# Two attentions of a transformer block run inside the weight products of other branches instead of after them

## The reference, cut to what matters

```python
h = rms_norm(x, norm_mix_pre[i]);  z = h @ w_in[i]
c_q, c_kv, k_rope, q_c, k_c, v_c, g_a, g_b, g_c = jnp.split(z, split_points, axis=-1)
o_a = mla_attention(c_q, c_kv, k_rope, positions, mla_q_norm[i], w_uq[i], mla_kv_norm[i], w_ukv[i])
o_b = fourier_mix(h)
o_c = windowed_gqa(q_c, k_c, v_c, positions, gqa_sink[i])
merged = (jax.nn.sigmoid(g_a) * (o_a @ w_branch_a[i])
          + jax.nn.sigmoid(g_b) * (o_b @ w_branch_b[i])
          + jax.nn.sigmoid(g_c) * (o_c @ w_branch_c[i]))
# mla_attention: q = rms_norm(c_q) @ w_uq, 8 heads of 64 plain + 32 rotary channels;
#   kv = rms_norm(c_kv) @ w_ukv; one rotary key k_rope for all heads; softmax over all 512 keys
# windowed_gqa: 8 query heads, 2 key heads of 64 channels, a band of 128 tokens to each side, a sink
# apply_rope: (t1*cos - t2*sin, t1*sin + t2*cos) over the two halves of the rotary channels
```

## Time and profile before

| | before |
|---|---|
| runs | 3261.25, 3264.87, 3265.0 us |
| median | 3264.87 us |
| the profiled execution | 3264.1 us, of which the span is 3262.3 us |
| PE busy | 3083.3 us (95%) |
| granted TensorE clock, mean | 0.973 |

### The profile page before, as it was taken

The page is one execution under the profiler, slowest core; times in us unless marked ns, Lnnn a source line. Parts: engine busy times, 40 slices in busy tenths (PEclk is TensorE's granted clock), DMA queues, the critical chain, the costliest instruction groups (busy, mean ns, idle before and its releaser), DMA issues.

```text
span 3262.3 us, 42020 instructions
## 1 busy us (share of the span) xinstructions
PE 3083.3 (95%) x15048; PEld 2478.3 (76%) x15048; DVE 1220.6 (37%) x2009; ACT 1294.8 (40%) x2023; POOL 1493.3 (46%) x879
## 2 busy tenths in 40 slices
PE   8989998999989989998999979889999998899999
PEld 6866686888867856686888869858788876688887
DVE  5344433222053445434221070453555115645510
ACT  3353543222243353543222243464555326344421
POOL 3366454444444456355444453353444433344442
PEclk9999999999999989999999999999999998899999
DMA  3212132333322213032333322201333332233322
GB/s 124 91 46 91 39 110 79 95 96 97 103 84 84 91 33 103 23 120 78 96 96 98 102 65 92 75 1 59 96 96 96 94 93 72 74 94 96 96 92 89
DMA packets 78522, 274.37 MB, mean 84 GB/s; under 512 B 8504, under 2 KB 12216, under 8 KB 78400
## 3 DMA queue, kind: packets, MB, share of 16 engines
q1 hardware_dynamic: 74064, 266.05, 26.2%
q10 hardware_dynamic: 4336, 6.63, 0.6%
HBM read 270.54 MB, written 2.10 MB: 84 GB/s over the span
## 4 chain that ended last, share of the span: by engine, by line
PE 84%; DVE 7%; ACT 4%; issue 2%; POOL 2%; DMA 1%; DVEq 0%; ACTq 0%; SPq 0%; POOLq 0%
PE ps L583 24%; PE ps L585 24%; PE ps L584 24%; PE ps L809 3%; PE ps L822 2%; DVE HL L1587 1%; PE ps L845 1%; PE ps L948 1%; PE ps L949 1%; PE ps L950 1%; PE ps L659 1%; DVE ps L1576 1%; DVE X L1579 1%; POOL WLO L2030 1%; DMA WRAW<-wall 1%
## 5 line engine op out<-in xcount | busy, mean ns | idle before, releaser
L2030 POOL TENSOR_TENSOR WLO<-WRAW,WHI 128x1024 fp32r<-128x1024 f32 x471 | 1137.5, 2419 | 1341.0 <-ACT WHI L1114 1340.3
L583 PE MATMUL ps<-HH,WHI 128*128 128x512 f32 x2288 | 904.7, 395 | 50.9 <-DVE HL L1587 23.9
L584 PE MATMUL ps<-HL,WHI 128*128 128x512 f32 x2288 | 897.2, 392 | 0.0
L585 PE MATMUL ps<-HH,WLO 128*128 128x512 f32 x2288 | 896.9, 392 | 0.0
L1114 ACT ACTIVATE WHI<-WRAW 128x1024 fp32r<-128x1024 f32 x471 | 494.8, 1052 | 401.5 <-DMA WRAW<-wall 401.5
L583 PEld LDWEIGHTS ps<-HH,WHI 128*128 128x128 f32 x2288 | 432.9, 189 | 159.7 <-issue 23.1
L585 PEld LDWEIGHTS ps<-HH,WLO 128*128 128x128 f32 x2288 | 433.5, 189 | 92.4
L584 PEld LDWEIGHTS ps<-HL,WHI 128*128 128x128 f32 x2288 | 433.8, 190 | 87.9
L1924 DVE SCALAR_TENSOR_TENSOR ps<-U,COLS,ps 128x512 f32<-128x512 f32 x208 | 157.0, 755 | 153.9 <-ACT ps L1430 138.7
L1610 DVE TENSOR_TENSOR ACC<-ACC,SQ 128x512 f32<-128x512 f32 x80 | 73.8, 922 | 317.8 <-ACT SQ L1299 303.2
L585 PE MATMUL ps<-F2H,WLO 128*128 128x512 f32 x384 | 151.7, 395 | 0.0
(11 more groups left out here) (353 smaller groups left out, 4769.9 us busy)
## 6 DMA issues: line engine op xcount, KB each, us to landing
WRAW<-wall SPq DMA_DIRECT2D x502, 512.0 KB, 3.6
DFT<-dft ACTq DMA_DIRECT2D x4, 516.0 KB, 5.4
XROWS<-xin SPq DMA_DIRECT2D x2, 1024.0 KB, 7.2
y<-YROWS ACTq DMA_DIRECT2D x4, 512.0 KB, 2.6
PROWS<-pin ACTq DMA_DIRECT2D x2, 512.0 KB, 3.8
DIL<-dil ACTq DMA_DIRECT2D x1, 768.0 KB, 5.3
COLS<-cols ACTq DMA_DIRECT2D x1, 294.5 KB, 6.7
POSI<-posi SPq DMA_DIRECT2D x1, 256.0 KB, 11.5
```

The lines of the kernel that those rows point to most:

```text
L583: pe.matmul(out_, WHI[w_at], x_hi, start=first, stop=False)
L584: pe.matmul(out_, WHI[w_at], x_lo, start=False, stop=False)
L585: return pe.matmul(out_, WLO[w_at], x_hi, start=False, stop=last)
L2030: pool.tensor_tensor(WLO[:, s, :], whole, WHI[:, s, :].bitcast(F32), ALU.subtract).then_inc(wt_lo, 1)
```

## The change

`attention` gets a second form, `carried`, in which its pairs are woven into a host stage.

- The gqa attention is carried by `fourier_branch`. The stage has 19 steps. Step q makes the scores of pair q, the value products of pair q - 3, and turns pair q - 2. In even steps up to 14 a gate tile is made (two of its 8 parts before the turning, six after it), in odd ones the mirrored tile. Steps 16 and 17 hold the first gate tile of the `branch` stage that comes next (`begun`).
- The mla attention is carried by a new stage `branch_mla` of 19 steps, which holds the six other tiles of o_c: half a gate tile, half a gate tile, and a tile over the four tiles of OC, in turns.
- The scores have one pair of PSUM banks (4 and 5) instead of two, the value products one bank, and the tiles rotate over three banks instead of four. The turned probabilities have 4 slots instead of 8. Results of the groups wait in `OCR`, `OCR2`, `OAR` (copied by DVE, `heads_out`) and are split at the stage's end (`heads_hi`, `heads_lo`), since the operand's place is still in use by the host.
- The gates in the host stages are made with Tanh (x 0.5, then (1 + t) x 0.5) instead of Sigmoid.
- The squares of CQ, their sum, factors and rows (`cq_square`, `cq_sums`, `cq_spread`) are made inside `fourier_branch`. The operand stages of CQ keep the rounding and the remainder.
- `w_uq` is packed with the rotary columns of each head twice, the second time with the halves exchanged, so each head's product has 128 rows; the rows 64 to 127 of RBQ are multiplied once with a table that holds the cosine and the signed sine. The keys hold the rotated `k_rope` twice. The scores contract over 128 rows. What is left of `rope` is the key's part, and it stands ahead of `mla_heads`.

```diff
-            u.append(("w_uq", l, 0, Q_LORA, n * 2 * MLA_QK, 2 * MLA_QK))
+            u.append(("w_uq doubled", l, 0, Q_LORA, n * 2 * MLA_QK, 2 * P))
...
         f = add("fourier", tiles=2 * ST + 2 * FGROUPS + 1, per={"channels_transformed": 8, "tokens_transformed": 9, "operand_hi_ready": 8, "dft_loaded": 32, "nyquist_cleared": 2, "nyquist_loaded": 16}, op=op, made=start, l=l)
-        fb = add("fourier_branch", units=2 * DT, tiles=3 * DT, per={"weights_folded": 2 * DT, "gate_ready": DT, "unfolded": DT, "product_ready": DT}, made=f)
-        fb.att = attention("gqa", GQA_H // 2, "OC", l=l, proj=pr)
+        cq = add("cq_norms", per={"cq_square_ready": QT + 1, "cq_square_added": QT - 1, "cq_summed": 1, "cq_mean_ready": 2, "cq_factors_ready": 1, "cq_spread": 2, "cq_rows_ready": 2}, proj=pr)
+        fb = add("fourier_branch", units=2 * DT, tiles=4 * DT, per={"weights_folded": 2 * DT, "gate_ready": DT, "unfolded": DT, "product_ready": DT}, made=f)
+        attention("gqa", GQA_H // 2, "OC", l=l, proj=pr, made=fb)
         fb.tables = tables
         need_oc = need(GQA_H // 2)
-        operand("CQ", "CQ", f"mla_q_norm{l}", QT, True, made=pr)
-        nq = norm("Q", Q_LORA, "inner")
-        operand("CQ", "CQ", f"mla_kv_norm{l}", 1, True, t=QT, made=pr)
-        nk = norm("K", KV_LORA, "inner")
+        fb.cq = cq
+        operand("CQ", "CQ", f"mla_q_norm{l}", QT, False, made=pr)
+        operand("CQ", "CQ", f"mla_kv_norm{l}", 1, False, t=QT, made=pr)
         need_cq = need(QT + 1)
-        branch(GQA_H // 2, "OC", False, False, need_oc, (nq, nk), reps=1)
-        heads = add("mla_heads", units=5, tiles=20, per={"part_multiplied": 4 + 11}, op=need_cq)
-        rp = add("rope", tiles=MLA_H + 1, per={"rope_rotated": 9, "cos_applied": 9, "rope_added": 9, "rope_keys_spread": 1}, proj=pr, heads=heads)
-        branch(GQA_H // 2, "OC", False, False, need_oc, reps=3, t=2)
-        attention("mla", MLA_H // 2, "OA", l=l, rope=rp)
+        fb.proj = branch(GQA_H // 2, "OC", False, False, need_oc, reps=1)
+        fb.proj.begun = True
+        rp = add("rope", tiles=1, per={"rope_rotated": 1, "cos_applied": 1, "rope_added": 1, "rope_keys_doubled": 1, "rope_keys_spread": 1}, proj=pr)
+        heads = add("mla_heads", units=5, tiles=20, per={"part_multiplied": 4 + 11, "rope_scaled": 1}, op=need_cq, made=cq)
+        bm = add("branch_mla", units=2 * (DT - 2), tiles=16, per={"gate_ready": DT - 2, "product_ready": DT - 2}, kt=GQA_H // 2, src="OC", op=need_oc, t=2)
+        attention("mla", MLA_H // 2, "OA", l=l, rope=rp, made=bm)
+        bm.att.qk = heads
         branch(MLA_H // 2, "OA", False, True)
...
+            def fourier_branch(st):
+                att, after = st.att, st.proj
+                attention_ready(att)
+                for q in range(att.heads * ST + DEPTH + 1):
+                    n, odd = divmod(q, 2)
+                    if q < att.heads * ST:
+                        scores(att, q)
+                    if q > DEPTH:
+                        value_products(att, q - DEPTH - 1)
+                    if n < DT and not odd:
+                        tile_part(st, 2 * n, 3 * n, pair["H"], DT, 0, 2)
+                    if DEPTH <= q < att.heads * ST + DEPTH:
+                        turn(att, q - DEPTH)
+                    if n < DT and not odd:
+                        tile_part(st, 2 * n, 3 * n, pair["H"], DT, 2, DT)
+                    elif n < DT:
+                        mirrored(st, n)
+                    elif q == 2 * DT:
+                        tile_part(after, 0, 0, pair["H"], DT, 0, 3)
+                        cq_sums(st.cq, att)
+                    elif q == 2 * DT + 1:
+                        tile_part(after, 0, 0, pair["H"], DT, 3, DT)
+                cq_spread(st.cq)
+
+            def cq_sums(st, att):
+
+                pe.wait_ge(*scores_free(att, att.heads * ST))
+                pe.wait_ge(S["cq_square_added"], st.at("cq_square_added", QT - 1))
+                pe.wait_ge(S["cq_square_ready"], st.at("cq_square_ready", QT + 1))
+                for x, at in ((ACC[:, :], 0), (SQ[:, 0, :], ST)):
+                    for s in range(ST):
+                        mm = pe.matmul(ps[4][:, at + s:at + s + 1], x[:, s * P:(s + 1) * P], ONES[:, 0:1], start=True, stop=True)
+                mm.then_inc(S["cq_summed"], 1)
+
+            def cq_spread(st):
+
+                pe.wait_ge(S["cq_factors_ready"], st.at("cq_factors_ready", 1))
+                for bank, at in ((5, 0), (4, ST)):
+                    for s in range(ST):
+                        mm = pe.transpose(ps[bank][:, s * P:(s + 1) * P], RC["Q"][:, at + s:at + s + 1].to_broadcast([P, P]), IDENT[:, :])
+                    mm.then_inc(S["cq_spread"], 1)
 
...
+                pr = st.proj
+                pe.wait_ge(bank_free[st.bank(0)], st.use(0))
+                pe.wait_ge(bank_free[pr.bank(10)], pr.use(10) + 1)
+                pe.matmul(ps[st.bank(0)][0:MLA_QK, :], ROT[MLA_NOPE:MLA_QK, :], KRAW[MLA_NOPE:MLA_QK, :],
+                          start=True, stop=True).then_inc(S["rope_rotated"], 1)
...
+            def branch_mla(st):
+                att = st.att
+                attention_ready(att)
+                pe.wait_ge(S["operand_ready"], st.op + st.kt)
+                for q in range(att.heads * ST + DEPTH + 1):
+                    r, part_ = divmod(q, 3)
+                    if q < att.heads * ST:
+                        scores(att, q)
+                    if q > DEPTH:
+                        value_products(att, q - DEPTH - 1)
+                    if DEPTH <= q < att.heads * ST + DEPTH:
+                        turn(att, q - DEPTH)
+                    if r < DT - 2 and part_ < 2:
+                        tile_part(st, 2 * r, 2 * r, pair["H"], DT, 4 * part_, 4 * part_ + 4)
+                    elif r < DT - 2:
+                        tile_part(st, 2 * r + 1, 2 * r + 1, pair[st.src], st.kt, 0, st.kt)
 
...
+            def fourier_branch(st):
+                att = st.att
+                for q in range(att.heads * ST + DEPTH + 1):
+                    n, odd = divmod(q, 2)
+                    if q < att.heads * ST:
+                        exponentials(att, q)
+                    if DEPTH <= q < att.heads * ST + DEPTH:
+                        turned_copies(att, q - DEPTH)
+                    if q < 2 * DT:
+                        split_of(st, q)
+                    if q <= QT:
+                        cq_square(st.cq, q)
+                    if n < DT and not odd:
+                        act.wait_ge(bank_free[st.bank(3 * n)], st.use(3 * n) + 1)
+                        act.activation(GT[:, :], GT[:, :], ACT.Tanh, scale=0.5).then_inc(S["gate_ready"], 1)
+                    elif n < DT:
+                        k = 3 * n + 2
+                        act.wait_ge(unit_used, st.unit(2 * n + 1) + 1)
+                        if n >= 2:
+                            act.wait_ge(bank_free[st.bank(k - 7)], st.use(k - 7) + 1)
+                        act.activation(TM[:, n % 2, 0:UH], ps[st.bank(k)][:, 0:UH], ACT.Copy, scale=0.5).then_inc(bank_free[st.bank(k)], 1)
+                heads_hi(att, unit_used, st.unit(2 * DT - 1) + 1)
...
+            def heads_hi(att, done, at):
+
+                act.wait_ge(done, at)
+                for g in range(att.heads):
+                    if g < att.heads - 1:
+                        act.wait_ge(bank_free[att.made.heads_bank()], att.made.heads_use(g) + 1)
+                    else:
+                        act.wait_ge(S["pair_multiplied"], att.at("pair_multiplied", 4 * g + 4))
+                    x = raw_heads(att, g) if g < att.heads - 1 else out_bank(att, g)[:, :]
+                    act.activation(pair[att.out][0][:, g, :], x, ACT.Copy).then_inc(S["operand_hi_ready"], 1)
...
+                dve.wait_ge(S["cq_rows_ready"], st.made.at("cq_rows_ready", 2))
+                at = slice(MLA_NOPE, P)
+                dve.tensor_tensor(RBQ[at, :], RBQ[at, :], COS[at, :], ALU.mult).then_inc(S["rope_scaled"], 1)
+                dve.wait_ge(S["rope_scaled"], st.at("rope_scaled", 1))
...
+                dve.wait_ge(S["rope_rotated"], st.at("rope_rotated", 1))
+                dve.tensor_tensor(TM[at, 0, :], ps[st.bank(0)][at, :], SIN[at, :], ALU.mult).then_inc(bank_free[st.bank(0)], 1)
+                dve.tensor_tensor(KRAW[at, :], KRAW[at, :], COS[at, :], ALU.mult).then_inc(S["cos_applied"], 1)
+                dve.wait_ge(bank_free[st.bank(0)], st.use(0) + 1)
+                dve.wait_ge(S["cos_applied"], st.at("cos_applied", 1))
+                dve.tensor_tensor(KRAW[at, :], KRAW[at, :], TM[at, 0, :], ALU.add).then_inc(S["rope_added"], 1)
+                dve.wait_ge(S["rope_added"], st.at("rope_added", 1))
+                dve.tensor_copy(KRAW[MLA_QK:P, :], KRAW[at, :]).then_inc(S["rope_keys_doubled"], 1)
...
+            def fourier_branch(st):
+                att = st.att
+                pool.wait_ge(S["table_stepped"], st.tables.at("table_stepped", 16))
```

(64 more changed lines are left out.)

559 lines of the change are left out of this document (307 added, 252 removed).

## The result

| | before | after |
|---|---|---|
| median | 3263.06 us (4 runs, 3260.64 to 3265.0) | 3189.86 us (4 runs, 3188.47 to 3190.48) |
| ratio | | 0.9774, 95% interval 0.9762 to 0.9787 |
| the profiled execution | 3264.1 us, span 3262.3 | 3190.5 us, span 3188.6 |
| mean granted clock | 0.973 | 0.977 |

The change makes the kernel 73.2 us faster. Some of the 13 is the starting point, as the median of before is now 3263.06 and was 3264.87 when the forecast was made; the gain itself is 12 us larger than forecast. The 0.14 us alone would mean nothing (the four runs of after spread over 2 us), the 12 do.

A forecast was written before the change was run, and what follows sets the result against it. PE was taken as the bound (84% of the chain), losing time to idling and a halved clock; 3264.1 - 71.9 removed + 10.4 at joints = 3202.6, forecast 3203 us, range 3190 to 3236.

The forecast's parts named there:

- Rival 3: Its own statement is missing from the text; forecast together with rival 1 at 3212 to 3258 us, chance 0.25.
- Rivals 1 and 2: Queues late in every host step, 3222 or 3241 us, 0.25 with rival 3; VectorE and GpSimd contention, 3278 us, 0.09.
- the floor: From Fourier branch through mla attention, PE never waiting at full clock: 263.6 us a layer, 71.9 us saved in all.
- rival 5: Better than forecast: no waiting at the joints and none of the half clock, 3193 us or less; chance 0.05.
- joints at nothing, and 2 us of scaling error in the floor: Basis of the range's lower end, 3190 us: no new PE waits between stages, and a floor off by 2 us.
- the joints: Places between and at starts of stages where PE waits anew: 5.2 us a layer, 10.4 in all, between 0 and 25.
- The floor's gqa pair: Gqa in the Fourier host: 0.625 of an mla pair's 3.77 us by keys, so 2.35 us, 37.6 for 16.
- The fourth unit of the short stage: Short o_c stage: unit ready after 10.2 us, PE there after 8.3, so 1.9 us of waiting, between 0 and 3.
- The clock after it: Half clock behind the short o_c stage's wait: 1.7 us a layer, between 0 and 3.4.
- The fourth unit of the heads: Heads stage: unit ready after 14.6 us, PE there after 13.4, so 1.2 us of waiting, between 0 and 4.4.
- The rest: Starts, with a table load ahead of mla's first exponentials: 0.4 us a layer, between 0 and 1.5.
- The mla term: Mla attention stage: 67.1 us less 60.3 of PE work, so 6.8 us a layer lost and to be regained.

The follow-up runs named there:

- bias run: Each gqa bias tile made twice on POOL, against the kernel after: 3189.53 us, ratio 0.9776.
- same-half run: Both heads of a gqa pair read query and key rows from the same partition half, against the kernel after: 3205.81 us, ratio 0.9828.
- the run made for it: Three more ACT copies of 512 columns ahead of the rounding of the short o_c stage's fourth unit, against the kernel after: 3191.67 us, ratio 0.9784.
- mla apart: Mla attention in a stage of its own behind six uncarried o_c tiles, against the kernel after: 3196.13 us, ratio 0.9801.
- 96-row run: Scores over the first 96 of 128 rows, against the kernel with mla apart: 3199.75 us, ratio 0.9806.

## Why the prediction was right in kind and off in size

**The mechanism** held: both attentions, the norms and rope left the path, PE never starved in the hosts, and the clock stayed at 1.00. The mla host took 110.5 us against 110. Rival 3 fell with the rows: one table load of 1.28 us in each host. Rivals 1 and 2 have nothing in the waits, and the bias run shows that there was slack left. The weaving paid what the floor said, and more; the case that came true is rival 5, which had a chance of 0.05.

**The failed step is the one that set the range's lower end: "joints at nothing, and 2 us of scaling error in the floor".** The stretch was to last 263.6 + 5.2 = 268.8 us a layer and lasted 262.6, below the floor itself. Of these 6.2 us, 4.1 lie in the joints (1.07 us a layer for 5.2) and 2.1 in a floor that was too high:

- *The floor's gqa pair, "0.625 of that: 2.35 us".* The Fourier host took 113.3 us for 116.5. Less the Fourier branch (70.4), a gate tile (5.5) and the sums and spread (2.5, for my 3.0), 34.9 are left, 2.18 a pair. I scaled a pair of mla by its keys, and so missed that gqa's heads lie in different row halves and their scores overlap. The value matmuls that I compared work with all 128 rows in both attentions and couldn't show it; the scores in the same chain of before, 0.85 us, could. The same-half run shows the overlap, 16 to 17 us over both layers, and also that scaling by columns is itself too cheap: without overlap a score group takes 1.06 and 1.49 us, where it gave 0.86 and 1.29. That a pair came out no further off is luck: its scores take 0.74 us on average for my 1.08, but the pair 2.18 for 2.35, so its other pieces cost more than scaled and took back half. That is 2.7 us a layer, with 0.5 more from the sums; the short stage, the heads and the mla host took 1.1 more than the floor gave them. The pair alone, 5.4 us in both layers, is over the 2 us that I allowed.
- *The fourth unit of the short stage, 1.9.* It waited 0.93. The four roundings and two rows on ACT took 3.5 us for 4.2, and the last remainder on DVE some 0.8 for 1.2; a table load of 1.28 us on ACT, which I hadn't seen coming, fell into the wait for DVE.
- *"The clock after it", 1.7.* It never fell, not behind 0.93 us nor behind 2.12 in the run made for it. In the kernel before the norms lost their clock over three waits (1.27, 1.36 and 1.35 us, of which I counted two) and 16 records of one-column sums in 24.1 us; I carried half of that loss to one wait.
- *The fourth unit of the heads, 1.2.* No wait. POOL had its three remainders done in 7.1 us from 251.65 on, ahead of PE. The bound of nothing was the right one.
- *The rest*, 0.4 for mla's start, came to 0.14.

Over both layers that is 8.3 us in the joints and 4.2 in the floor, 12.5 together, for the 12 us by which the gain was larger than forecast.

**Contention of DVE and POOL** came out other than weighed, and the trace says why. Groups by form of the Fourier host after, for DVE's fold, POOL's probabilities, and DVE's product:

```profile
L1794 DVE TENSOR_TENSOR WF<-WRAW 128x512 f32<-128x512 f32 x14 | 11.5, 858 | 2.6 <-DMA WRAW<-wall 2.6
...
L2344 POOL TENSOR_SCALAR SG<-SG,RS 128x384 f32<-128x384 f32 x10 | 7.9, 801 | 2.5 <-DVE RS L2008 2.5
...
L1819 DVE SCALAR_TENSOR_TENSOR MG<-GT,MG 128x512 f32<-128x512 f32 x8 | 5.8, 730 | 0.1
```

The fold rose from 679 ns to 858, far from the 1992 that I gave it as a worst case, and POOL's scaling from 584 to 801. The product fell from 1992 to 730. Which POOL instruction runs beside it decides. A product before, with POOL; a product after, with POOL; and, also after, the cosine product of the key and the sum behind it, with POOL:

```profile
143.79 1.84 DVE L1659 TENSOR_TENSOR MG<-MG,SG 128x512 f32<-128x512 f32 x1
142.67 2.41 POOL L2030 TENSOR_TENSOR WLO<-WRAW,WHI 128x1024 fp32r<-128x1024 f32 x1 [1.01 <-ACT WHI L1114]
...
154.43 0.72 DVE L1819 SCALAR_TENSOR_TENSOR MG<-GT,MG 128x512 f32<-128x512 f32 x1
154.03 2.10 POOL L2344 TENSOR_SCALAR SGX<-SGX,RS 128x384 f32<-128x384 f32 x2 [0.27 <-DVE RS L2008]
...
243.42 2.17 DVE L1958 TENSOR_TENSOR KRAW<-KRAW,COS 32x512 f32<-32x512 f32 x1
245.69 0.68 DVE L1961 TENSOR_TENSOR KRAW<-KRAW,TM 32x512 f32<-32x512 f32 x1
234.81 10.23 POOL L2262 TENSOR_TENSOR WLO<-WRAW,WHI 128x1024 fp32r<-128x1024 f32 x4 [10.86 <-ACT WHI L1216]
```

Before, all seven products of the earlier trace rows began while a remainder of POOL ran, which reads two tensors, and took 1.82 to 2.40 us. After, seven of the eight met only POOL's scaling, which reads one, and took 0.67 to 0.72; the eighth shared its first 0.44 us with a remainder and took 0.99. The new form of the product (one scalar and two tensors) isn't needed to explain it: after, too, a product of two tensors took 2.17 us beside a remainder, and the sum of the same shape 0.68 once POOL had stopped at 245.04. So what I wrote down as the price of POOL's work is that of its remainders, the folds beside its scaling and bias tiles rose by a quarter only, and by luck the weaving parted the products from the remainders. POOL was busy for 80.9 us where the sums of before gave 69.4, still 71% of the stage.

**Credits, part by part** (us over both layers, forecast and run): gqa 21.0 and 23.7; norms 14.6 and 16.7; rope 21.6 and 22.7; mla 13.6 and 6.3. The joints, forecast at 10.4 and found at 2.1, are no item beside these: each run already has the joints that its order leaves. The mla term was right as the loss of the old stage and wrong as a gain of *carrying*. From before to after, the six o_c tiles and mla together went from 49.77 + 67.09 us to 110.52, 6.3 a layer for my 6.8 less 0.4 at the start. But the separate stage with the wider tiles lasts 64.4 us and not 67.1, as the halved clock is gone there too. So of 12.7 us in both layers 7.1 come with the carrying (the stretches with mla apart), 3.6 with the step from 96 to 128 rows, and some 2 are in neither: the stages of before, 67.1 us in both layers, are that much longer than the 66.9 and 65.4 of the 96-row run, almost all in layer 1, where the clock stayed low for longer.

## What to carry to other kernels

Weaving a latency-bound attention into a stage of plain products gives back idle time and clock together; the floor (the stage's own work on PE, at full clock) is then a good forecast, if the slack of the other queues is counted per step. Take such a floor from rows of the very matmuls, which the trace of before often has, and scale only between matmuls of the same geometry: a pair of operands in different row halves is cheaper than its columns say. Price a joint at the wait that the queues give, and add the clock only where the rows show it behind a single wait of that kind, with the same shapes ahead of it. Price the meeting of two engines by the pair of instructions that will meet, not by how busy the other engine is.

## What the runs showed of the hardware

- Two float32 score matmuls over 64 rows, one in each half of the rows: 0.84 us with 384 columns each, against 1.49 in the same half; 0.63 with 256 columns, against 1.06.
- A VectorE product of two float32 tensors in SBUF, 512 columns: 1.82 to 2.40 us when begun beside GpSimd's subtraction of two tensors, 0.67 to 0.72 (in the form with a scalar) beside its scaling of one tensor. On 32 partitions 2.17 us beside the subtraction, where a sum of the same shape took 0.68 with GpSimd idle.
- Behind the same idle time of 2.85 us the granted clock fell to 1.2 GHz where the matmuls ahead worked with 96 rows (six stages) and stayed at 2.4 GHz where they worked with 128 (two stages). One wait of 2.12 us between products of 128 rows left it at 2.4 GHz as well.
